# ScalarE forms the modulated norm in place with scale and shift, VectorE multiplies and subtracts 512 wide

## The chip, the core and the metric

The kernel runs on one core of a Trainium2 chip. The metric is the device time of one execution in microseconds, the median of several runs. The engines that matter here: TensorE multiplies matrices, VectorE and ScalarE work element by element on tiles of 128 partitions, and SyncE issues the transfers from memory. They run side by side and wait for each other through semaphores.

## What is computed

Two transformer blocks. The first has six sublayers ("subs" 0 to 5: feed-forward, differential attention, feed-forward, feed-forward, grouped attention, feed-forward), each of them on 256 tokens of `x` and, but for the last, 256 tokens of a context. Every sub begins with the same operation, and this is the one that is changed:

```python
def rmsnorm(x, g):
    xf = x.astype(jnp.float32)
    y = xf * lax.rsqrt(jnp.mean(xf * xf, axis=-1, keepdims=True) + NORM_EPS)
    return (y * g.astype(jnp.float32)).astype(x.dtype)

def modulated_norm(h, g, m, k):
    return rmsnorm(h, g) * (1.0 + m[..., k + 1, :]) + m[..., k, :]

def half_ffn(h, m, k, g_pre, g_post, w_in, w_out):
    y = swiglu(modulated_norm(h, g_pre, m, k), w_in, w_out)
    return gated_residual(h, y, g_post, m, k, 0.5)
```

`m` comes from the condition of `x` or of the context, so scale and shift differ between the two halves of the tokens. A second block of two layers follows; its norms have code of their own.

## The kernel before

Activations lie with the 1024 features on partitions, in eight chunks (KC) of 128, and the tokens along the row: 512 (TT), of which the first 256 (S) are `x` and the others the context. `hT` is the residual stream, `uT` the norm's product, `rstd` the root's inverse for each token, `modA` the columns of scale (norm weight times one plus the scale), `modt` the columns of shift. Each f32 matrix product is made of three with operands split into a high and a low part: `u_hi` with `w_hi`, `u_lo` with `w_hi`, `u_hi` with `w_lo` (lines 407 to 409). Weights stream through a ring of four slots; ScalarE makes `w_hi` of each half slot (line 943), VectorE `w_lo` (line 1354), and this frees the slot for SyncE. Two halves of weights ("columns") are ready before a sub begins.

The order of the work is written out by hand, engine by engine, and a sub starts like this. ScalarE squares `hT`, TensorE sums the squares (line 491), ScalarE makes `rstd` (lines 934 and 935). Then VectorE in `pre` walks over pieces of 256 tokens: it writes `uT` as `hT` times `modA` times `rstd` (line 1380) and, three pieces behind, `u_lo` as `uT` plus shift minus `u_hi` (line 1369). Scale and shift are different for `x` and context, hence two pieces a chunk. ScalarE in `modulate` writes `u_hi` as `uT` plus shift, rounded (line 976). TensorE in `two_columns` takes chunk by chunk for two columns of weights at once, and waits for each chunk's `u_lo`: 48 products. Subs 0 to 3 form and multiply all 512 tokens, sub 4 forms 512 but multiplies the first 256 in these two columns, sub 5 has 256 tokens only and one piece a chunk. After `modulate` ScalarE goes on with `w_hi` and the sub's own work, VectorE with `w_lo` and the condition's products (line 1342).

Of the kernel before, what the change touches and what calls it, by code (L numbers as in the profile page):

```python
# [7 lines left out]
F32 = mybir.dt.float32  # L8
F32R = mybir.dt.float32r
ACT = mybir.ActivationFunctionType  # L10
ALU = mybir.AluOpType
# [4 lines left out]
KC = D // P  # L16
S = 256
TT = 2 * S
DEPTH = 2
# [101 lines left out]
        _n += _w  # L121
NTABS, NHTABS = sum(TABS.values()), sum(HTABS.values())

T_READY_END = 5 * 2 * KC + KC + KC * (DEPTH + 1)

ADDED = KC - 3

# [6 lines left out]
def program(nc, wk, x_in, cols_in, crow_in, tabs_in, htabs_in, trig_in, uk_in, uv_in, out):  # L134
    with ExitStack() as ctx:
        def sem(name):
            return ctx.enter_context(nc.semaphore(name))
# [6 lines left out]
        def place(region, name, cols, dtype=F32):  # L144
            t = nc.alloc_sbuf_tensor_at(name, [P, cols], dtype, offset=at[region])
            at[region] += (cols * 4 + 31) // 32 * 32
            return t
# [5 lines left out]
        hT = place("fixed", "hT", KC * TT)  # L153
# [8 lines left out]
        modt = place("fixed", "modt", 6 * 48)  # L162
        modA = place("fixed", "modA", 6 * 16)
        modC = place("fixed", "modC", 6 * 16)
        small = place("fixed", "small", 256)
        rstd = place("fixed", "rstd", TT)
# [4 lines left out]
        u_hi = place("first", "u_hi", KC * TT, F32R)  # L171
        u_lo = place("first", "u_lo", KC * TT, F32R)
        uT = place("first", "uT", KC * TT)
# [88 lines left out]
        mod_ready = sem("mod_ready")  # L262
# [2 lines left out]
        ss_done = sem("ss_done")  # L265
        rstd_ready = sem("rstd_ready")
        t_ready = sem("t_ready")
        u_ready = sem("u_ready")
        ulo_ready = sem("ulo_ready")
        hhi_ready = sem("hhi_ready")  # L270
# [47 lines left out]
        def half_hi(h, a, b):  # L318
            n = (h % NW) * HALF
            return w_hi[:, n + a:n + b]  # L320

        def half_lo(h, a, b):
            n = (h % NW) * HALF
            return w_lo[:, n + a:n + b]
# [22 lines left out]
        def _(sp):  # L347
# [44 lines left out]
            assert n == NSLOTS  # L392
            sp.wait_ge(t_ready, T_READY_END)
            sp.dma_start(out, uT[:, 0:KC * S]).then_inc(out_done, 16)
# [3 lines left out]
        def _(pe):  # L398
# [6 lines left out]
            def three(bank, hi, lo, x_hi, x_lo, first, last):  # L405

                mm(bank, hi, x_hi, start=first, stop=False)  # L407
                mm(bank, hi, x_lo, start=False, stop=False)  # L408
                return mm(bank, lo, x_hi, start=False, stop=last)  # L409

            def weights(h):
                pe.wait_ge(wlo_ready, h + 1)

            def bank_a():

                nonlocal a
                if a >= 2:
                    pe.wait_ge(a_free, a - 1)
                a += 1
                return bankA[(a - 1) % 2]  # L420

            def bank_v():

                nonlocal v
                if v >= 2:
                    pe.wait_ge(v_free, v - 1)
                v += 1
                return bankV[(v - 1) % 2]

            def column(bank, T, xh, xl, stride, ready=None, seen=0, per=1):  # L430

                nonlocal H
                for k in range(KC):
                    if ready is not None:
                        pe.wait_ge(ready, seen - (KC - 1 - k) * per)
                    at_k = slice(k * stride, k * stride + T)
                    last = three(bank[:, 0:T], half_hi(H, k * P, (k + 1) * P), half_lo(H, k * P, (k + 1) * P),
                                 xh[:, at_k], xl[:, at_k], k == 0, k == KC - 1)
                last.then_inc(half_done, 1)
                H += 1  # L440
# [19 lines left out]
            def two_columns(banks, T, xh, xl, stride, ready, seen, per=1):  # L460

                nonlocal H
                weights(H + 1)
                for k in range(KC):
                    pe.wait_ge(ready, seen - (KC - 1 - k) * per)
                    at_k = slice(k * stride, k * stride + T)
                    for b in range(2):
                        last = three(banks[b][:, 0:T], half_hi(H + b, k * P, (k + 1) * P),
                                     half_lo(H + b, k * P, (k + 1) * P), xh[:, at_k], xl[:, at_k], k == 0, k == KC - 1)
                        if k == KC - 1:  # L470
                            last.then_inc(half_done, 1)
                H += 2
# [26 lines left out]
                    norm_term(c, T, ready, seen, src, stride)  # L499

            def ffn_in(T, f):
                two_columns([bank_a(), bank_v()], T, u_hi, u_lo, TT, ulo_ready, ulo_seen, T // S)
                for j in range(1, FT):
                    weights(H)
                    column(bank_a(), T, u_hi, u_lo, TT)
                    weights(H)
                    column(bank_v(), T, u_hi, u_lo, TT)
# [144 lines left out]
            for sub in range(6):  # L652
                T = S if sub == 5 else TT
                norm_sum(T, sq_ready, sq_seen)
                sq_seen += KC
                ulo_seen += KC * (T // S)
                if sub in FFN_SUBS:
                    f = FFN_SUBS.index(sub)
                    ffn_in(T, f)
                    ffn_out(T)  # L660
                    continue
                first = a
                two_columns([bank_a(), bank_a()], S if sub == 4 else T, u_hi, u_lo, TT, ulo_ready, ulo_seen, T // S)
                if sub == 1:
                    project(14, TT)
                    for s in range(4):
# [29 lines left out]
                else:  # L696
# [3 lines left out]
                    for t in range(10):  # L700
                        w = S if t < 8 else TT
                        n = t * S if t < 8 else GA_K + (t - 8) * TT
# [6 lines left out]
                    for t in range(10):  # L709
                        n = t * S if t < 8 else GA_K + (t - 8) * TT  # L710
# [209 lines left out]
        def _(act):  # L920
            f = nc.scalar.activation
# [45 lines left out]
                rms_inverse(rstd[:, 0:T], bankN[:, 0:T], D).then_inc(rstd_ready, 1)  # L967

            def modulate(sub, T):
                nonlocal t_seen  # L970
                for c in range(KC):
                    for s in range(T // S):
                        t_seen += 1
                        act.wait_ge(t_ready, t_seen)
                        piece = slice(c * TT + s * S, c * TT + (s + 1) * S)
                        f(u_hi[:, piece], uT[:, piece], ACT.Identity,
                          bias=modt[:, sub * 48 + 2 * c + s:sub * 48 + 2 * c + s + 1]).then_inc(u_ready, 1)

            def ffn(T, nth):
                nonlocal a, v, hid  # L980
# [106 lines left out]
            for sub in range(6):  # L1087
                T = S if sub == 5 else TT
                squares(T, h_ready if sub else None, h_seen - KC, 1)
                if sub == 0:  # L1090
# [5 lines left out]
                    high()  # L1096
                norm(T)
                modulate(sub, T)
                if sub == 0:
                    high()  # L1100
# [73 lines left out]
            for lay in range(DEPTH):  # L1174
# [78 lines left out]
                for h in range(SB_HEADS + 1):  # L1253
                    n = 8 * lay + h
# [14 lines left out]
                  scale=-1.0).then_inc(b2["mx"], 1)  # L1269
# [26 lines left out]
        def _(dve):  # L1296
            ts, tt, stt = nc.vector.tensor_scalar, nc.vector.tensor_tensor, nc.vector.scalar_tensor_tensor
            H = K = a = v = parts = 0
            steps = norms = 0
            t_n = u_n = rots = hns = units = hids = 0  # L1300
# [57 lines left out]
            def pre(sub, T):  # L1358
                nonlocal norms, t_n, u_n
                norms += 1  # L1360
                dve.wait_ge(mod_ready, sub + 1)
                dve.wait_ge(rstd_ready, norms)

                def low_part(j):
                    c, s = divmod(j, T // S)
                    dve.wait_ge(u_ready, u_n + j + 1)
                    piece = slice(c * TT + s * S, c * TT + (s + 1) * S)
                    shift = modt[:, sub * 48 + 2 * c + s:sub * 48 + 2 * c + s + 1]
                    stt(u_lo[:, piece], uT[:, piece], shift, u_hi[:, piece].bitcast(F32),  # L1369
                        ALU.add, ALU.subtract).then_inc(ulo_ready, 1)  # L1370

                behind = 3
                pieces = KC * (T // S)
                for j in range(pieces):
                    c, s = divmod(j, T // S)
                    if j >= behind:
                        low_part(j - behind)
                    n = c * TT + s * S
                    k = sub * 16 + 2 * c + s
                    stt(uT[:, n:n + S], hT[:, n:n + S], modA[:, k:k + 1], rstd[:, s * S:(s + 1) * S],  # L1380
                        ALU.mult, ALU.mult).then_inc(t_ready, 1)
                    t_n += 1
                for j in range(pieces - behind, pieces):
                    low_part(j)
                u_n += pieces

            def post(sub, T):
                nonlocal norms, yrs
# [177 lines left out]
            for sub in range(6):  # L1566
                T = S if sub == 5 else TT
                pre(sub, T)
                if sub == 0:
                    low()  # L1570
# [36 lines left out]
                else:  # L1607
                    lows(8 + 2 + 2)
                    dve.wait_ge(trig_ready, 32)
                    for t in range(10):  # L1610
                        w = S if t < 8 else TT
                        n = t * S if t < 8 else GA_K + (t - 8) * TT
                        b = (t % 2) * TT
                        head_norm(mix[:, n:n + w], col("gaq" if t < 8 else "gak"), hr[:, b:b + w])
                    for t in range(10):
                        n = t * S if t < 8 else GA_K + (t - 8) * TT
# [17 lines left out]
            for lay in range(DEPTH):  # L1634
# [7 lines left out]
                behind = 2  # L1642
# [261 lines left out]
            for c in range(KC):  # L1904
                stt(uT[:, c * S:(c + 1) * S], tile(hT, c), col("final", c), rstd[:, 0:S],
                    ALU.mult, ALU.mult).then_inc(t_ready, 1)
                t_n += 1
            assert t_n == T_READY_END
            assert H == K == HALVES
# [194 lines left out]
```

## Time and profile before

| | us |
|---|---|
| median of 3 runs | 2709.39 (2707.68 to 2712.68) |
| profiled execution | 2700.16 |
| its span | 2698.4 |
| TensorE busy in the span | 2490.8 (92%) |
| VectorE busy | 1612.1 (60%) |
| ScalarE busy | 1042.0 (39%) |
| mean granted TensorE clock | 0.961 of full speed |

The profiled execution is one run, recorded by the profiler; the span is the time from its first to its last instruction. Busy shares are means over stages that have different limits. A timeline gives for each instruction its start, its duration, and in brackets how long the engine was idle before it and what ended that. The duration of an instruction is longer than its place in a row of like ones, since the next starts before it has ended.

### The profile page before, as it was taken

To read this page: it belongs to the slowest core of one execution; us is meant where nothing else is said; L and a number is where in the kernel's file an instruction comes from. 1 tells how busy PE (TensorE), PEld (TensorE's weight loads), DVE (VectorE), ACT (ScalarE), POOL (GpSimd) and SP (SyncE) were. 2 spreads that over 40 slices of the span, in tenths; PEclk is the share of its full clock that TensorE was granted. 3 is DMA by queue.
4 is the path that set the end of the run, shared out by engine and by line. 5 is a ranking of instruction groups with operands and counts; after the bars stand their busy time and mean duration, and the time that the engine had idled before them with its cause. 6 is when DMAs were issued, how large, how long until landed. Compare 5 with 4: busy or idle time off the path is not lost.

```text
span 2698.4 us, 35057 instructions
## 1 busy us (share of the span) xinstructions
PE 2490.8 (92%) x14142; PEld 2105.3 (78%) x14142; DVE 1612.1 (60%) x2827; ACT 1042.0 (39%) x1739; POOL 0.2 (0%) x4
## 2 busy tenths in 40 slices
PE   6999998987899999899999888998998878998968
PEld 5888886874678888688888668998988658998658
DVE  8767755268477673676233655556466367466466
ACT  3222324247432223422232545445444434544433
POOL 0000000000000000000000000000000000000000
PEclk9999999989999999999999989999999879999879
DMA  6544441210135543145222203553544104534202
GB/s 267 209 190 187 187 156 63 89 53 1 67 135 197 197 189 125 47 187 203 94 94 98 90 32 116 188 188 141 183 140 170 63 16 143 209 141 156 79 1 95
DMA packets 48689, 349.72 MB, mean 130 GB/s; under 512 B 5392, under 2 KB 5520, under 8 KB 6544
## 3 DMA queue, kind: packets, MB, share of 16 engines
q1 hardware_dynamic: 48528, 347.48, 34.8%
q8 instruction: 113, 1.85, 0.3%
q14 instruction: 48, 0.39, 0.0%
HBM read 346.41 MB, written 1.05 MB: 129 GB/s over the span
## 4 chain that ended last, share of the span: by engine, by line
PE 84%; DVE 10%; ACT 3%; issue 2%; DMA 1%; SPq 0%; DVEq 0%; ACTq 0%
PE ps L407 24%; PE ps L409 24%; PE ps L408 24%; PE ps L491 1%; PE ps L571 1%; PE ps L573 1%; PE ps L572 1%; PE ps L614 1%; DVE small L1516 1%; DVE w_lo L1354 1%; PE ps L601 1%; DVE conv L1715 1%; ACT w_hi L943 1%; DVE yT L1394 1%; PE ps L794 1%
## 5 line engine op out<-in xcount | busy, mean ns | idle before, releaser
L943 ACT ACTIVATE w_hi<-ring 128x1024 fp32r<-128x1024 f32 x504 | 533.8, 1060 | 1261.4 <-PE ps L409 1187.4
L1354 DVE TENSOR_TENSOR w_lo<-ring,w_hi 128x1024 fp32r<-128x1024 f32 x504 | 616.6, 1224 | 634.9 <-ACT w_hi L943 632.7
L407 PE MATMUL ps<-u_hi,w_hi 128*128 128x512 f32 (+1 forms) x1744 | 631.7, 362 | 29.6 <-DVE u_lo L1369 27.2
L409 PE MATMUL ps<-u_hi,w_lo 128*128 128x512 f32 (+1 forms) x1744 | 635.1, 364 | 0.0
L408 PE MATMUL ps<-u_lo,w_hi 128*128 128x512 f32 (+1 forms) x1744 | 632.9, 363 | 0.0
L407 PEld LDWEIGHTS ps<-u_hi,w_hi 128*128 128x128 f32 x1744 | 330.3, 189 | 89.2 <-issue 32.6
L408 PEld LDWEIGHTS ps<-u_lo,w_hi 128*128 128x128 f32 x1744 | 330.3, 189 | 56.0 <-issue 0.5
L409 PEld LDWEIGHTS ps<-u_hi,w_lo 128*128 128x128 f32 x1744 | 330.2, 189 | 48.8
L407 PE MATMUL ps<-uh,w_hi 128*128 128x256 f32 x1184 | 336.5, 284 | 30.2 <-ACT zt L1231 17.0
L1342 DVE CUSTOM_DVE_ANT_0 waste<-ring,condb,cols 128x1024 f32<-128x1024 f32 x280 | 346.5, 1279 | 8.2 <-DMA ring<-in_wk 8.2
L408 PE MATMUL ps<-ul,w_hi 128*128 128x256 f32 x1184 | 333.1, 281 | 0.0
L409 PE MATMUL ps<-uh,w_lo 128*128 128x256 f32 x1184 | 333.1, 281 | 0.0
L409 PE MATMUL ps<-h_hi,w_lo 128*128 128x512 f32 (+1 forms) x704 | 257.2, 365 | 0.0
L407 PE MATMUL ps<-h_hi,w_hi 128*128 128x512 f32 (+1 forms) x704 | 255.8, 363 | 0.5 <-DVE h_lo L1426 0.5
L408 PE MATMUL ps<-h_lo,w_hi 128*128 128x512 f32 (+1 forms) x704 | 256.1, 364 | 0.0
L407 PEld LDWEIGHTS ps<-uh,w_hi 128*128 128x128 f32 x1184 | 225.7, 191 | 36.7 <-DVE w_lo L1354 20.0
L408 PEld LDWEIGHTS ps<-ul,w_hi 128*128 128x128 f32 x1184 | 225.9, 191 | 0.0
L409 PEld LDWEIGHTS ps<-uh,w_lo 128*128 128x128 f32 x1184 | 225.9, 191 | 0.0
L1440 DVE TENSOR_TENSOR hidden<-ps,hidden 128x512 f32<-128x512 f32 (+1 forms) x88 | 55.0, 625 | 202.9 <-PE ps L409 202.9
L407 PEld LDWEIGHTS ps<-h_hi,w_hi 128*128 128x128 f32 x704 | 132.1, 188 | 23.8 <-issue 0.9
L408 PEld LDWEIGHTS ps<-h_lo,w_hi 128*128 128x128 f32 x704 | 132.1, 188 | 23.8 <-issue 0.7
L409 PEld LDWEIGHTS ps<-h_hi,w_lo 128*128 128x128 f32 x704 | 132.3, 188 | 19.7
(274 smaller groups left out, 2711.1 us busy)
## 6 DMA issues: line engine op xcount, KB each, us to landing
ring<-in_wk SPq DMA_DIRECT2D x324, 1024.0 KB, 4.8
hT<-in_x SPq DMA_DIRECT2D x1, 2048.0 KB, 17.7
htabs<-in_htabs SPq DMA_DIRECT2D x1, 1152.0 KB, 7.2
condb<-in_crow SPq DMA_DIRECT2D x1, 1024.0 KB, 5.2
out_t<-uT SPq DMA_DIRECT2D x1, 1024.0 KB, 3.9
trig<-in_trig SPq DMA_DIRECT2D x3, 256.0 KB, 5.0
wuk<-in_uk SPq DMA_DIRECT2D x2, 256.0 KB, 5.2
wuv<-in_uv SPq DMA_DIRECT2D x2, 256.0 KB, 5.4
```

What stands on the lines that cost most here:

```text
L407: mm(bank, hi, x_hi, start=first, stop=False)
L408: mm(bank, hi, x_lo, start=False, stop=False)
L409: return mm(bank, lo, x_hi, start=False, stop=last)
L491: last = mm(bankN[:, 0:T], tab("ones"), src[:, c * stride:c * stride + T], start=c == 0, stop=c == KC - 1)
L571: mm(bank, x_h, half_hi(h, n, n + 256), start=k == 0, stop=False)
L572: mm(bank, x_l, half_hi(h, n, n + 256), start=False, stop=False)
L573: last = mm(bank, x_h, half_lo(h, n, n + 256), start=False, stop=k == KC - 1)
L601: last = nc.tensor.transpose(ps[5 + u % 2][:, kt * P:(kt + 1) * P], specs[u]["prob"](u % 2, kt), tab("ident"))
L943: f(half_hi(K, 0, HALF), ringed(n, K % 2 * HALF, (K % 2 + 1) * HALF), ACT.Copy).then_inc(whi_ready, 1)
L1342: last = nc.vector.tensor_tensor_reduce(waste[:, c * D:(c + 1) * D], ringed(slot, t * D, (t + 1) * D), condb[:, c * D:(c + 1) * D], 1.0, c ...
L1354: tt(half_lo(K, 0, HALF), ringed(HALF_SLOT[K], K % 2 * HALF, (K % 2 + 1) * HALF), half_hi(K, 0, HALF).bitcast(F32), ALU.subtract).then_inc ...
L1440: tt(h, bankV[v % 2][:, 0:T], h, ALU.mult).then_inc(v_free, 1)
```

## The change

ScalarE now does the whole affine step: for each piece of 256 it writes `uT` in place, scale times `uT` plus shift, and one chunk behind it copies the 512 of a chunk into `u_hi`, rounded. VectorE multiplies `hT` by `rstd` for a whole chunk and, two chunks behind, subtracts `u_hi` from `uT` for a whole chunk. A new semaphore `u_whole` keeps ScalarE's copy behind its own pieces. TensorE's waits count chunks instead of pieces. In sub 5 a chunk is 256 wide, so there the number of ScalarE's instructions doubles and VectorE's stays.

```diff
-T_READY_END = 5 * 2 * KC + KC + KC * (DEPTH + 1)
+T_READY_END = 6 * KC + KC * (DEPTH + 1)
...
-                two_columns([bank_a(), bank_v()], T, u_hi, u_lo, TT, ulo_ready, ulo_seen, T // S)
+                two_columns([bank_a(), bank_v()], T, u_hi, u_lo, TT, ulo_ready, ulo_seen)
...
-                ulo_seen += KC * (T // S)
+                ulo_seen += KC
...
             def modulate(sub, T):
+
                 nonlocal t_seen
-                for c in range(KC):
-                    for s in range(T // S):
+                act.wait_ge(mod_ready, sub + 1)
+                for c in range(KC + 1):
+                    if c < KC:
                         t_seen += 1
                         act.wait_ge(t_ready, t_seen)
-                        piece = slice(c * TT + s * S, c * TT + (s + 1) * S)
-                        f(u_hi[:, piece], uT[:, piece], ACT.Identity,
-                          bias=modt[:, sub * 48 + 2 * c + s:sub * 48 + 2 * c + s + 1]).then_inc(u_ready, 1)
+                        for s in range(T // S):
+                            piece = slice(c * TT + s * S, c * TT + (s + 1) * S)
+                            k = 2 * c + s
+                            f(uT[:, piece], uT[:, piece], ACT.Identity, bias=modt[:, sub * 48 + k:sub * 48 + k + 1],
+                              scale=modA[:, sub * 16 + k:sub * 16 + k + 1]).then_inc(u_whole, 1)
+                    if c:
+
+                        act.wait_ge(u_whole, sub * 2 * KC + c * (T // S))
+                        chunk = slice((c - 1) * TT, (c - 1) * TT + T)
+                        f(u_hi[:, chunk], uT[:, chunk], ACT.Copy).then_inc(u_ready, 1)
...
-                def low_part(j):
-                    c, s = divmod(j, T // S)
-                    dve.wait_ge(u_ready, u_n + j + 1)
-                    piece = slice(c * TT + s * S, c * TT + (s + 1) * S)
-                    shift = modt[:, sub * 48 + 2 * c + s:sub * 48 + 2 * c + s + 1]
-                    stt(u_lo[:, piece], uT[:, piece], shift, u_hi[:, piece].bitcast(F32),
-                        ALU.add, ALU.subtract).then_inc(ulo_ready, 1)
-
-                behind = 3
-                pieces = KC * (T // S)
-                for j in range(pieces):
-                    c, s = divmod(j, T // S)
-                    if j >= behind:
-                        low_part(j - behind)
-                    n = c * TT + s * S
-                    k = sub * 16 + 2 * c + s
-                    stt(uT[:, n:n + S], hT[:, n:n + S], modA[:, k:k + 1], rstd[:, s * S:(s + 1) * S],
-                        ALU.mult, ALU.mult).then_inc(t_ready, 1)
-                    t_n += 1
-                for j in range(pieces - behind, pieces):
-                    low_part(j)
-                u_n += pieces
+                def low_part(c):
+                    dve.wait_ge(u_ready, u_n + c + 1)
+                    chunk = slice(c * TT, c * TT + T)
+                    tt(u_lo[:, chunk], uT[:, chunk], u_hi[:, chunk].bitcast(F32), ALU.subtract).then_inc(ulo_ready, 1)
+
+                behind = 2
+                for c in range(KC + behind):
+                    if c < KC:
+                        n = c * TT
+                        tt(uT[:, n:n + T], hT[:, n:n + T], rstd[:, 0:T], ALU.mult).then_inc(t_ready, 1)
+                        t_n += 1
+                    if c >= behind:
+                        low_part(c - behind)
+                u_n += KC
```

ScalarE at the start of sub 0, before: from the root (`rstd`) over the sixteen pieces of `u_hi` to the next weights.

```order
L934 ACTIVATE rstd<-ps,cols 128x512 [waits ss_done]
L935 ACTIVATE rstd<-rstd 128x512 [waits act_step]
L976 ACTIVATE u_hi<-uT,modt 128x256 [waits t_ready] x16
L943 ACTIVATE w_hi<-ring 128x1024 [waits w_ready2]
L981 ACT_TABLE_LOAD
```

The same place of the changed kernel; the group of two pieces and a copy stands there six times more where the dots are.

```order
L935 ACTIVATE rstd<-ps,cols 128x512 [waits ss_done]
L936 ACTIVATE rstd<-rstd 128x512 [waits act_step]
L981 ACTIVATE uT<-uT,modt,modA 128x256 [waits t_ready,mod_ready]
L981 ACTIVATE uT<-uT,modt,modA 128x256
L981 ACTIVATE uT<-uT,modt,modA 128x256 [waits t_ready]
L981 ACTIVATE uT<-uT,modt,modA 128x256
L987 ACTIVATE u_hi<-uT 128x512 [waits u_whole]
...
L987 ACTIVATE u_hi<-uT 128x512 [waits u_whole] x2
L944 ACTIVATE w_hi<-ring 128x1024 [waits w_ready2]
```

The first `u_hi` was the first instruction behind the root; now it is the fifth.

VectorE at the same place, before: the end of the weights' low parts, then products and low parts in turn.

```order
L1354 TENSOR_TENSOR w_lo<-ring,w_hi 128x1024 [waits whi_ready] x2
L1380 SCALAR_TENSOR_TENSOR uT<-hT,modA,rstd 128x256 [waits mod_ready,rstd_ready,x_ready,dve_step]
L1380 SCALAR_TENSOR_TENSOR uT<-hT,modA,rstd 128x256 x2
L1369 SCALAR_TENSOR_TENSOR u_lo<-uT,modt,u_hi 128x256 [waits u_ready]
L1380 SCALAR_TENSOR_TENSOR uT<-hT,modA,rstd 128x256
```

And in the changed kernel:

```order
L1364 TENSOR_TENSOR w_lo<-ring,w_hi 128x1024 [waits whi_ready] x2
L1383 TENSOR_TENSOR uT<-hT,rstd 128x512 [waits mod_ready,rstd_ready,x_ready,dve_step]
L1383 TENSOR_TENSOR uT<-hT,rstd 128x512 x2
L1377 TENSOR_TENSOR u_lo<-uT,u_hi 128x512 [waits u_ready]
L1383 TENSOR_TENSOR uT<-hT,rstd 128x512
```

The pattern is the same, three products ahead of the first low part, but each instruction is a chunk of 512 and no longer a piece of 256.

## Rows read from the trace of the kernel before

**Rows 1.** The page: the span, and the engines' shares of the last chain.

```profile
span 2698.4 us, 35057 instructions
...
PE 84%; DVE 10%; ACT 3%; issue 2%; DMA 1%; SPq 0%; DVEq 0%; ACTq 0%
```

**Rows 2.** Waits: who waited for whom, us in total, times, longest.

```profile
PE ps L407 <- DVE u_lo L1369: 27.2, 10, 5.5
```

**Rows 3.** Timeline of sub 1: start, duration, engine, line, out<-in, count [idle before].

```profile
429.44 1.28 DVE L1380 SCALAR_TENSOR_TENSOR uT<-hT,modA,rstd 128x256 f32<-128x256 f32 x3 [1.33 <-ACT rstd L935]
429.96 1.30 ACT L976 ACTIVATE u_hi<-uT,modt 128x256 fp32r<-128x256 f32 x3 [0.63 <-DVE uT L1380]
...
431.42 0.48 DVE L1369 SCALAR_TENSOR_TENSOR u_lo<-uT,modt,u_hi 128x256 fp32r<-128x256 f32 x1
...
432.05 0.47 PE L407 MATMUL ps<-u_hi,w_hi 128*128 128x512 f32 x1 [4.11 <-DVE u_lo L1369]
...
434.16 0.63 PE L407 MATMUL ps<-u_hi,w_hi 128*128 128x512 f32 x1
...
435.44 0.63 PE L407 MATMUL ps<-u_hi,w_hi 128*128 128x512 f32 x1
...
436.47 0.40 PE L407 MATMUL ps<-u_hi,w_hi 128*128 128x512 f32 x1
...
440.93 1.27 DVE L1369 SCALAR_TENSOR_TENSOR u_lo<-uT,modt,u_hi 128x256 fp32r<-128x256 f32 x3
...
444.03 0.39 PE L407 MATMUL ps<-u_hi,w_hi 128*128 128x512 f32 x1
444.23 1.06 ACT L943 ACTIVATE w_hi<-ring 128x1024 fp32r<-128x1024 f32 x1 [2.68 <-PE ps L409]
```

**Rows 4.** TensorE by stretches of sub 1: stretch, length, busy, granted clock, DMA.

```profile
429.40:432.70 3.30, 0.65 (x3) 1.00 0.55 233
432.80:436.10 3.30, 3.30 (x9) 0.50 0.00 0
436.20:444.70 8.50, 8.50 (x38) 1.00 0.01 2
```

**Rows 5.** Timeline of VectorE: two 512-wide multiplies by the root.

```profile
730.41 1.29 DVE L1394 TENSOR_TENSOR yT<-yT,rstd 128x512 f32<-128x512 f32 x2 [2.55 <-ACT rstd L935]
```

**Rows 6.** ScalarE by line: ns min/median/max, first and last start; then a timeline row.

```profile
L976 ACT ACTIVATE u_hi<-uT,modt x88: 492/509/512, 44.4 to 1672.1; 128x256 fp32r<-128x256 f32 x88
...
L1183 ACT ACTIVATE uh<-conv x16: 416/418/419, 1870.1 to 2287.0; 128x256 fp32r<-128x256 f32 x16
...
L1203 ACT ACTIVATE pad<-ps x16: 363/365/368, 1928.0 to 2357.7; 128x256 f32<-128x256 f32 x16
...
L1035 ACT ACTIVATE yT<-ps,modC x24: 456/458/471, 686.3 to 1655.1; 128x256 f32<-128x256 f32 x24
...
L1125 ACT ACTIVATE u_hi<-uT x8: 612/612/632, 671.4 to 682.8; 128x512 fp32r<-128x512 f32 x8
...
686.29 0.82 ACT L1035 ACTIVATE yT<-ps,modC 128x256 f32<-128x256 f32 x2
```

**Rows 7.** Timeline of sub 4: first piece, last low parts, the last two chunks' products.

```profile
1514.31 1.28 DVE L1380 SCALAR_TENSOR_TENSOR uT<-hT,modA,rstd 128x256 f32<-128x256 f32 x3 [1.32 <-ACT rstd L935]
...
1525.79 1.28 DVE L1369 SCALAR_TENSOR_TENSOR u_lo<-uT,modt,u_hi 128x256 fp32r<-128x256 f32 x3
...
1526.34 0.38 PE L407 MATMUL ps<-u_hi,w_hi 128*128 128x256 f32 x1 [0.61 <-DVE u_lo L1369]
...
1527.15 0.37 PE L407 MATMUL ps<-u_hi,w_hi 128*128 128x256 f32 x1
```

**Rows 8.** Timeline around sub 5: 256-wide multiplies, first piece, first product.

```profile
1657.63 0.76 DVE L1394 TENSOR_TENSOR yT<-yT,rstd 128x256 f32<-128x256 f32 x2 [1.12 <-ACT rstd L935]
...
1666.86 1.27 DVE L1380 SCALAR_TENSOR_TENSOR uT<-hT,modA,rstd 128x256 f32<-128x256 f32 x3 [3.77 <-ACT rstd L935]
...
1668.68 0.55 PE L407 MATMUL ps<-u_hi,w_hi 128*128 128x256 f32 x1 [2.88 <-DVE u_lo L1369]
```

More of the change, by code:

```diff
@@ L267, in program @@
         t_ready = sem("t_ready")
+        u_whole = sem("u_whole")
         u_ready = sem("u_ready")
@@ L662, in _ @@
                 first = a
-                two_columns([bank_a(), bank_a()], S if sub == 4 else T, u_hi, u_lo, TT, ulo_ready, ulo_seen, T // S)
+                two_columns([bank_a(), bank_a()], S if sub == 4 else T, u_hi, u_lo, TT, ulo_ready, ulo_seen)
                 if sub == 1:
```

## The prediction

> **What bounds the kernel now.** I read the chain that ended last first: TensorE carries 84% of it and VectorE 10% [rows 1], so a change on ScalarE and VectorE counts only where TensorE stands and waits for them. The table of waits then says where that is for this code: TensorE waited for `u_lo` (line 1369) ten times, 27.2 us in all, the longest 5.5 us [rows 2]. That is the whole stake of the change: six norms ("subs" 0 to 5), each with a start-up before TensorE's first product, and nothing else.
>
> The timeline of sub 1 shows one such start-up [rows 3]. Take T0 = 429.44, when VectorE starts its first piece of `uT`. Sixteen pieces of `uT` and sixteen of `u_lo`, each 256 wide, follow each other; from the second `u_lo` (431.42) to the fourteenth (440.93) are 24 places in 9.51 us, 0.396 us a place, 1.58 us a chunk of 512. TensorE's first product needs both halves of chunk 0: the second `u_lo` ends at 431.42 + 0.48 = 431.90 and the product starts at 432.05, so T0 + 2.61, 0.15 us behind its input. From there on TensorE never waits in subs 0 to 3: it works through 48 products without a gap. Three products take 435.44 - 434.16 = 1.28 us at a granted clock of 0.50, 0.427 each; 33 products take 444.03 - 436.47 = 7.56 us at full clock, 0.229 each, or 1.37 us a chunk [rows 3, 4]. The clock stood at 1.2 GHz for a stretch just after the start, following the 4.11 us in which TensorE idled, and at 2.4 GHz before and after [rows 3, 4]. ScalarE had 2.68 us of idle time when the two columns ended [rows 3]: what it does later is covered, its first results are not.
>
> **The change, part by part.** The norm's multiply on VectorE: before 2 x 256 wide, now one instruction of 512. The like of it is `yT<-yT,rstd`, two in 1.29 us, one of them some 0.69: a place of 0.60 [rows 5]. `u_lo` becomes an instruction of the same kind and size. VectorE so needs 1.20 us a chunk for 1.58; over the program 176 places of 0.396 give way to 80 of 0.60 and, in sub 5, 16 of 0.34 (two in 0.76 [rows 8]), 69.7 us to 53.4, 16 less. All of that is idle time won, since VectorE no longer sets the pace.
>
> ScalarE before: two pieces a chunk, `Identity` with the shift as a column from memory, 0.509 us each. After: two pieces with two such columns (shift and scale), written in place, and a plain copy of 512, which takes 0.612 [rows 6]. No row has an instruction with both columns. Rows have each alone: a bias column makes 0.418 (plain, SBUF to SBUF) into 0.509, +0.091; a scale column makes 0.365 (plain, from PSUM) into 0.458, +0.093 [rows 6]. If they add, a piece takes 0.60; if the second comes free, 0.51. Back to back such instructions overlap: two of 0.458 end after 0.82, so the place is 0.36, 0.096 less than the duration [rows 6]. The place of a new piece is then 0.50, or 0.41 (taken as 0.40) if the second column is free, and that of the copy 0.52. I take 0.50, since each column shows its own increment and no row shows one that came without; 0.40 stays for the range.
>
> The Trainium skill (ScalarE: Activation LUTs, What ACT_TABLE_LOAD costs) says that each pointer operand adds about 93 ns, and gives no discount for a second. The trace agrees for each alone and shows no pair. By that rule the change costs the 6.5 us below; without it, the 4.0 us of the first rival.
>
> Start-up of a 512-wide sub, from T0: VectorE's first multiply 0.68, hand-over to ScalarE 0.04 (429.44 to 429.96 is 0.52 with a piece of 0.48 [rows 3]), so ScalarE starts at 0.72. It now makes the two pieces of chunk 0, and, as the loop is written, the two of chunk 1 before the copy of chunk 0: 0.72 + 4 x 0.50 = 2.72. The copy ends at 3.33, VectorE starts the subtraction at 3.37 (its own third multiply is over at 1.9), ends at 4.06, and TensorE starts at 4.21. Before it was 2.61: **1.60 us later**. With 0.40 the same sum gives 3.81, 1.20 later.
>
> Pace behind it: ScalarE 2 x 0.50 + 0.52 = 1.52 us a chunk, TensorE 1.37 at best. The last chunk's `u_lo` comes at 4.21 + 6 x 1.52 + 0.60 = 13.93. VectorE's loop keeps two chunks behind: copy c lets it subtract (0.65 after the copy's start), then multiply chunk c+3 (0.60 and 0.72 more), 1.97 in all; ScalarE wants that at 2.04. The new loop just holds with 0.50; with 0.40 it sets 1.39 a chunk.
>
> *Subs 0 to 3* (512 wide, TensorE never out of input). Starting 1.60 later costs 1.60 if the clock's slow stretch moves along. If the stretch stays where it is, TensorE misses 1.60 us of slow time, 3.7 products at 0.427, and makes them up at full clock: 3.7 x 0.229 = 0.85. So 0.85 to 1.60 each, 1.22 taken; four subs: **+4.9** (3.4 to 6.4).
>
> *Sub 4* forms 512 but multiplies only 256 wide, so TensorE is faster than its input there and waits (0.61 us before the seventh chunk); the last chunk's products start at 1527.15, T0 + 12.84 [rows 7]. Now 13.93: **+1.1**. With 0.40: 3.81 + 6 x 1.39 + 0.60 = 12.75, -0.1. This is the one place where the faster VectorE could pay, and at 0.50 it doesn't.
>
> *Sub 5* (256 wide, one piece a chunk): TensorE started at T0 + 1.82 [rows 8]. Now the multiply takes 0.42, ScalarE starts at 0.46, two pieces to 1.46, copy 0.42, hand-over 0.04, subtraction 0.42, and 0.15: 2.49, **0.67 later**, 0.37 of it left if the slow stretch stays; 0.5 taken. With 0.40: 0.47 later, 0.35 taken.
>
> The new wait on `u_whole` asks for the chunk before the one just formed, whose pieces ended at least two pieces earlier; `mod_ready` VectorE awaits itself ahead of its first multiply, so it is there by then. Queued behind the `u_whole` wait is ScalarE's copy alone, and VectorE and TensorE wait for that copy anyway. I put both waits at nothing. If the wait took the overlap of 0.1 from each copy, sub 4 would lose 0.7 more and the others 0.1 each. DMA queues are not touched: the ring is released by `w_lo`, and its order is unchanged.
>
> Sum: 4.9 + 1.1 + 0.5 = 6.5 us on the profiled 2700.16, so 2706.7; the three timed runs have a median of 2709.39 with the same program, hence **2715.9 us**. Within this case the ends are 3.4 + 1.1 + 0.4 = 4.9 and 6.4 + 1.1 + 0.7 = 8.2: 2714.3 to 2717.6.
>
> **Rivals.** *The second column is free* (0.40 a piece). 1.20 later in subs 0 to 3, between 0.64 and 1.20 each: 3.7; sub 4 -0.1; sub 5 +0.35; sum 4.0, **2713.4 us**, no difference that can be told. For it: nothing in the rows excludes that two columns are fetched together. Against: the two increments are equal and each is the full one.
>
> *More slow clock.* TensorE's idle time before its first product grows from 4.11 us to 5.7 us in subs 0 to 4, and a slow stretch costs (0.427 - 0.229) x 8 products, 1.6 us, where it lies on products. Three to five more of these, here or in the gaps further on that the delay shifts, give 6.5 + 4.8 to 8.0: 2720.7 to 2723.9, say **2722 us**. For it: every start-up seen has such a stretch after its idle time. Against: one longer gap need not make two.
>
> *Faster, by less slow clock elsewhere.* The same program gave 2700.16 us profiled and 2707.68 to 2712.68 timed; something of that size moves with where the idle gaps fall. If the new spacing removed slow stretches, each gives 1.6 us back; the point is at 5 of them (6.5 us) for no change and 8 for faster by 0.2%: **2703 us**. Within the six norms themselves nothing can do that: the least the change costs there is zero, as the last chunk comes no sooner than before unless a piece's place is under 0.40. I see no row that speaks for so many.
>
> **How the numbers follow.** The forecast gets 0.55, the free column 0.2, more slow clock 0.2, less 0.05. What a measurement can tell from no change is about 0.2%, 5.4 us. The forecast's own span lies to nine tenths above 2714.8; part of it falls under that line with the spread of the medians, some 2 us. Slower: 0.55 x 0.7 + 0.2 x 0.3 + 0.2 x 0.95, 0.63, put at 0.6; faster 0.04; same 0.36. The range runs from the free column with its stretches at the low end and a median 1.5 us low (2709.5) to more slow clock (2723).
>
> **What would show it.** In the changed profile: ScalarE's piece 0.60 (0.51 in the first rival), first `uT` to first product 4.2 us in subs 0 to 4 (before 2.61), ScalarE's place a chunk 1.52; VectorE's busy time some 16 us lower; TensorE's wait for `u_lo` at about 27 + 5 x 1.6 + 0.7 = 36 us; its clock lines for the number of slow stretches. I am wrong if the piece takes 0.51 or if the spans of subs 0 to 3 grow by less than 0.8 us each, and in another way if the total moves by several us while these six places move as said: then it is the clock.

## The result

The changed kernel takes 2715.66 us (median of 13 runs, 2713.34 to 2719.29); the kernel before, in 13 runs, 2707.68 us. The ratio is 1.0031 with a 95% interval of 1.0021 to 1.0042: slower by 8.4 us (5.7 to 11.4). Beside the first experiments below, on one chip with them, the same file came out at 1.0043 (1.0024 to 1.0061). The forecast was 2715.9 us, slower. How much of that nearness is luck stands below, in the part on the prediction.

Behind what follows stand two profiled executions, 2700.16 us of before (span 2698.4) and 2713.34 us of after (span 2711.6). That of before lies 7.5 us under its median, so their difference of 13.2 us is more than the 8.0 of the medians. Their stages can be compared, their totals less so.

The page of the changed kernel, counterpart of [rows 1]: span, busy time by engine, and the shares of the last chain.

```profile
span 2711.6 us, 35031 instructions
...
PE 2492.2 (92%) x14142; PEld 2109.5 (78%) x14142; DVE 1599.1 (59%) x2747; ACT 1065.7 (39%) x1787; POOL 0.2 (0%) x4
...
PE 84%; DVE 9%; ACT 4%; issue 2%; DMA 1%; SPq 0%; DVEq 0%; ACTq 0%
```

VectorE is busy 13.0 us less than before, ScalarE 23.7 us more, and the chain has moved a point from the one to the other. The waits of the changed kernel (us in total, times, longest), counterpart of [rows 2]:

```profile
PE ps L408 <- DVE u_lo L1377: 35.3, 8, 7.6
DVE u_lo L1377 <- ACT u_hi L987: 18.7, 39, 1.5
ACT uT L981 <- DVE uT L1383: 7.0, 6, 2.8
```

TensorE waits 8.1 us longer for `u_lo`. VectorE, which never waited for `u_hi` before, does so 39 times now, while ScalarE waits for `uT` only at the six starts: ScalarE sets the pace. The timeline of sub 1, counterpart of [rows 3]:

```profile
431.45 1.90 DVE L1383 TENSOR_TENSOR uT<-hT,rstd 128x512 f32<-128x512 f32 x3 [1.31 <-ACT rstd L936]
432.23 2.08 ACT L981 ACTIVATE uT<-uT,modt,modA 128x256 f32<-128x256 f32 x4 [0.89 <-DVE uT L1383]
434.22 0.61 ACT L987 ACTIVATE u_hi<-uT 128x512 fp32r<-128x512 f32 x1
434.74 1.08 ACT L981 ACTIVATE uT<-uT,modt,modA 128x256 f32<-128x256 f32 x2
434.86 0.69 DVE L1377 TENSOR_TENSOR u_lo<-uT,u_hi 128x512 fp32r<-128x512 f32 x1 [1.52 <-ACT u_hi L987]
...
435.70 0.76 PE L408 MATMUL ps<-u_hi,w_hi 128*128 128x512 f32 x1 [5.74 <-DVE u_lo L1377]
435.72 0.61 ACT L987 ACTIVATE u_hi<-uT 128x512 fp32r<-128x512 f32 x1
```

T0 is 431.45. Four pieces stand ahead of the first copy, which starts at 434.22, T0 + 2.77; VectorE has waited 1.52 us for it; the first product starts at T0 + 4.25 where it was T0 + 2.61. The next copy starts at 435.72: 1.50 us a chunk.

What this is worth at the end of each norm is in the next table. The first column of each pair is the start of TensorE's first product, the second the end of the 48th (its start plus its duration), both from T0.

| sub | before | after | first later by | 48th later by |
|---|---|---|---|---|
| 0 | 2.61, 15.69 | 4.25, 17.63 | 1.64 | 1.94 |
| 1 | 2.61, 15.45 | 4.25, 16.98 | 1.64 | 1.53 |
| 2 | 2.61, 15.44 | 4.26, 18.10 | 1.65 | 2.66 |
| 3 | 2.61, 15.43 | 4.25, 17.04 | 1.64 | 1.61 |
| 4 | 2.61, 13.78 | 4.25, 14.88 | 1.64 | 1.10 |
| 5 | 1.82, 9.12 | 2.53, 11.11 | 0.71 | 1.99 |

The six sum to 10.8 of the spans' 13.2 us. The rest lies in the other work: from T0 of sub 1 to T0 of sub 2 the changed kernel takes 314.68 us for 314.28, though its norm costs 1.53, so there 1.1 us came back; between the norms of subs 4 and 5 it loses 1.3 us more than sub 4's norm costs, and behind the norm of sub 5 another 2.2. Two single profiles can't say whether these pieces belong to the change.

In subs 0, 2 and 5 the loss is larger than the later start. Sub 2 of the changed kernel on TensorE, by stretches (length, busy, granted clock, DMA), counterpart of [rows 4], and its products:

```profile
746.20:749.60 3.40, 0.00 (x0) 0.94 0.01 2
750.50:755.20 4.70, 4.70 (x11) 0.50 0.00 0
755.40:764.00 8.60, 8.60 (x38) 0.97 0.00 0
```

```profile
750.39 0.76 PE L408 MATMUL ps<-u_hi,w_hi 128*128 128x512 f32 x1 [5.74 <-DVE u_lo L1377]
...
755.22 0.63 PE L410 MATMUL ps<-u_hi,w_lo 128*128 128x512 f32 x1
755.64 0.57 PE L408 MATMUL ps<-u_hi,w_hi 128*128 128x512 f32 x1
...
763.84 0.39 PE L410 MATMUL ps<-u_hi,w_lo 128*128 128x512 f32 x1
```

The first twelve products, 750.39 to 755.64, ran at 1.2 GHz, 0.44 us each; before it were about eight [rows 3, 4]. The later start fell into a slow stretch that went on for longer. Sub 5 shows the same thing, before and after:

```profile
1668.70:1671.70 3.00, 3.00 (x14) 0.50 0.00 0
1672.00:1676.00 4.00, 4.00 (x36) 1.00 0.02 4
```

```profile
1678.60:1684.20 5.60, 5.60 (x27) 0.50 0.00 0
1684.60:1687.00 2.40, 2.40 (x23) 1.00 0.03 7
```

Before, the clock was up again by 1672.00, T0 + 5.1; after, it was still down at 1684.20, T0 + 8.3. How long the lower level lay on the 48 products follows from their length and mean granted clock (twice the length times what the mean lacks of 1): in subs 0 to 3 some 4.0, 3.4, 3.4 and 3.4 us before, 4.6, 2.9, 5.6 and 3.4 after, and in sub 5 3.1 and 6.0.

### The profile page after: what moved, and what is told of

It is laid out like the page before. It is cut to its first block, busy times and chain, and to the rows that moved or that the text cites. A ratio compares the mean times of both kernels' runs of the same rounds, so it can differ in the third digit from the quotient of the medians.

```text
span 2711.6 us, 35031 instructions
## 1 busy us (share of the span) xinstructions
PE 2492.2 (92%) x14142; PEld 2109.5 (78%) x14142; DVE 1599.1 (59%) x2747; ACT 1065.7 (39%) x1787; POOL 0.2 (0%) x4
## 3 DMA queue, kind: packets, MB, share of 16 engines
HBM read 346.41 MB, written 1.05 MB: 128 GB/s over the span
## 4 chain that ended last, share of the span: by engine, by line
PE 84%; DVE 9%; ACT 4%; issue 2%; DMA 1%; SPq 0%; DVEq 0%; ACTq 0%
PE ps L408 24%; PE ps L410 24%; PE ps L409 23%; PE ps L492 2%; PE ps L572 1%; PE ps L574 1%; PE ps L573 1%; PE ps L615 1%; DVE small L1518 1%; PE ps L602 1%; DVE w_lo L1364 1%; DVE conv L1717 1%; ACT w_hi L944 1%; PE ps L795 1%; ACT uT L981 1%
## 5 line engine op out<-in xcount | busy, mean ns | idle before, releaser
L408 PE MATMUL ps<-u_hi,w_hi 128*128 128x512 f32 (+1 forms) x1744 | 636.0, 365 | 37.7 <-DVE u_lo L1377 35.3
```

## The experiments

The theory: the change costs what TensorE's first product comes later at the start of each norm, with what the clock makes of it, and in sub 4 what the last chunk comes later. The first rival: ScalarE's pace or its longer work costs it. The second: each start tips the clock. Ratios are to the kernel before on the same chip; a thousandth is 2.7 us.

**The yardstick.** The changed file itself.

> The changed kernel once more, beside the others on the same chip. Theory 'start-up' (the change costs what TensorE's first product comes later in the six norms, and what the clock makes of it): +8 us on the kernel before, first product at T0 + 4.25 in subs 0 to 4. It is the yardstick for the others; no rival differs here.

1.0043 (1.0024 to 1.0061), +11.6 us (6.5 to 16.5), for 8 expected; first product at T0 + 4.25 in subs 0 to 4. The 48th products ended 2.41, 1.62, 2.72, 1.53, 1.10 and 1.96 us later than in the profile of before, 11.3 in all.

**The order of ScalarE's first three steps.**

```diff
-                    if c:
-                        act.wait_ge(u_whole, sub * 2 * KC + c * (T // S))
-                        chunk = slice((c - 1) * TT, (c - 1) * TT + T)
+                    for d in ([0] if c == 0 else [] if c == 1 else [c - 1]):
+                        act.wait_ge(u_whole, sub * 2 * KC + (d + 1) * (T // S))
+                        chunk = slice(d * TT, d * TT + T)
                         f(u_hi[:, chunk], uT[:, chunk], ACT.Copy).then_inc(u_ready, 1)
```

> The change, but ScalarE copies chunk 0 right behind its own two pieces instead of behind those of chunk 1; all later chunks as in the change. Theory 'start-up': the copy starts at T0 + 1.9 instead of 2.77, TensorE's first product at T0 + 3.4 instead of 4.25 in subs 0 to 4, 2.15 instead of 2.53 in sub 5; sub 4, which waits for its last chunk, gains nothing. 0.4 to 0.9 us less in subs 0 to 3 and 0.3 in sub 5: 2 to 4 us less than the change, +4 to +6 on before. Rival 'pace' (ScalarE's 1.5 us a chunk sets TensorE's progress): nothing gained, +8.

1.0021 (1.0006 to 1.0036), +5.7 us: 6 less than the yardstick, where 2 to 4 were expected, with intervals that overlap. Its timeline in sub 1:

```profile
431.46 1.89 DVE L1382 TENSOR_TENSOR uT<-hT,rstd 128x512 f32<-128x512 f32 x3 [1.66 <-ACT rstd L936]
432.24 1.09 ACT L981 ACTIVATE uT<-uT,modt,modA 128x256 f32<-128x256 f32 x2 [0.89 <-DVE uT L1382]
433.37 0.63 ACT L986 ACTIVATE u_hi<-uT 128x512 fp32r<-128x512 f32 x1
...
434.87 0.76 PE L408 MATMUL ps<-u_hi,w_hi 128*128 128x512 f32 x1 [4.90 <-DVE u_lo L1376]
```

The copy starts at T0 + 1.91, the first product at T0 + 3.41. In sub 4 the 48th product ended at 15.01 (14.88 in the change): an earlier start gains nothing where the last chunk decides. The six 48th products ended 1.67, 1.08, 0.91, 0.95, 1.23 and 1.56 us later than before, 7.4 in all for the yardstick's 11.3. That is 3.9 us less and inside the expected band; the difference of the medians alone would not carry it. The same instructions do the same work here, at the same pace; only the start differs, and the norms follow it. That speaks against the first rival, for which nothing would have been gained. The pace is not far away, though: in subs 2 and 3 of this run TensorE waited for `u_lo` at the seventh chunk (in sub 2 its weight load stood 0.28 us), so with this ScalarE loop the 48th product comes no sooner than about T0 + 16.35. In the four wide norms of the changed kernel's profile TensorE didn't wait once behind its first product: there the start decides.

**The second column.**

```diff
-                            f(uT[:, piece], uT[:, piece], ACT.Identity, bias=modt[:, sub * 48 + k:sub * 48 + k + 1],
-                              scale=modA[:, sub * 16 + k:sub * 16 + k + 1]).then_inc(u_whole, 1)
+                            f(uT[:, piece], uT[:, piece], ACT.Identity, bias=modt[:, sub * 48 + k:sub * 48 + k + 1]).then_inc(u_whole, 1)
```

> The change without the scale column in ScalarE's pieces (bias column only): the multiplication by norm weight and scale is left out of the computation. Theory 'each column has its own price': the piece falls from 0.587 to 0.51 us and its place from 0.49 to 0.41; first product at T0 + 3.9; sub 4's last chunk at 12.8 instead of 13.9, now set by VectorE's loop at 1.39 us a chunk. About 2 us less than the change, +6 on before. If both columns shared a price, the piece would stay at 0.587 and nothing would move.

This kernel leaves out the multiplication by norm weight and scale. 1.0032 (1.0020 to 1.0043), +8.7 us for 6 expected; beside the yardstick 3 less, within both intervals. The piece itself is clear. With both columns (the changed kernel), and with the shift's alone; columns are ns min/median/max, first and last start:

```profile
L981 ACT ACTIVATE uT<-uT,modt,modA x88: 583/587/602, 44.8 to 1682.1; 128x256 f32<-128x256 f32 x88
```

```profile
L981 ACT ACTIVATE uT<-uT,modt x88: 491/493/512, 44.7 to 1683.0; 128x256 f32<-128x256 f32 x88
```

The second column costs 0.094 us, as much as the first did in [rows 6]: they add. The first product came at T0 + 3.87 and sub 4's 48th ended at 13.85, 0.07 later than before. The other subs did not show it: 0.76, 2.30, 1.05, 2.35 and, in sub 5, 1.88 us later than before, with more slow clock in subs 1 and 3 (5.7 us of it on the 48 products for 3.4 before). This run settles the price of the instruction, not that of the program.

**The later start alone.** The kernel before, VectorE held ahead of its first piece; twice in the second file.

```diff
                 dve.wait_ge(rstd_ready, norms)
+                for wide in (512, 512, 64)[:3 if T == TT else 1] * 1:
+                    step(tt(u_lo[:, 7 * TT:7 * TT + wide], hT[:, 7 * S:7 * S + wide], rstd[:, 0:wide], ALU.mult))
```

> The kernel before with VectorE held up ahead of its first piece of every norm: three scratch multiplies (512, 512 and 64 wide, each awaited, about 1.6 us) in subs 0 to 4, one (0.7 us) in sub 5. Nothing of the change is in it. Theory 'start-up': TensorE's first product 1.6 us later as in the change, in sub 4 all 1.6 count: +8 to +10 on before, the change's loss to within 2 us. Rival 'pace' or 'ScalarE's longer work': at most the part of the start-up that products in the slow stretch don't absorb, under +4.

> As e3_later_once with twice the hold: about 3.2 us ahead of every norm in subs 0 to 4 and 1.4 us in sub 5, in all 17.6 us. Theory 'start-up, us for us, the clock averaged out': twice what e3_later_once cost (ratio 1.0055, 14.9 us), but no more than the hold plus some two slow stretches of 1.6 us: +15 to +21 on before. Rival 'a later start tips the clock': one more slow stretch in each of six norms, +25 or more. Rival 'products absorb it': under +10.

The hold in sub 1, once:

```profile
431.09 1.68 DVE L1364 TENSOR_TENSOR u_lo<-hT,rstd 128x512 fp32r<-128x512 f32 x3 [1.32 <-ACT rstd L935]
432.81 1.28 DVE L1382 SCALAR_TENSOR_TENSOR uT<-hT,modA,rstd 128x256 f32<-128x256 f32 x3
...
435.42 0.76 PE L407 MATMUL ps<-u_hi,w_hi 128*128 128x512 f32 x1 [5.81 <-DVE u_lo L1371]
```

It was 432.81 - 431.09 = 1.72 us, with 0.7 in sub 5 some 9.3 in all. Measured: once 1.0055 (1.0035 to 1.0076), +14.9 us (9.5 to 20.5); twice 1.0089 (1.0072 to 1.0105), +24.0 us (19.5 to 28.4). Both medians lie above the expected bands, 8 to 10 and 15 to 21; both intervals reach into them. By the medians the second hold added 9.1 us for 9.3 held, which the two intervals leave open by several us. The first added some 5 more than its length, though 9.5, the interval's low end, is next to none; in its profile the 48th products ended, beyond the hold, 0.11, 1.17, 1.13, -0.14, 0.01 and 1.31 us later, 3.6 in all, by the clock (in subs 1 and 2 it was down for 6.0 and 5.9 us of the 48 products, before for 3.4). In the profile of twice the hold they ended 0.10, 0.39, 0.37, 0.39, 0.01 and 0.62 us later beyond it, 1.9 in all: the longer idle time brought less slow clock into the norms than the shorter. The mean granted clock of the runs was 0.957 for once and 0.956 for twice, 0.960 and 0.961 for the kernel before beside them. So a later start, with nothing of the change in it, costs at least what it lasts. The change holds TensorE 1.64 us in five subs and 0.71 in the sixth, 8.9 us; with sub 4 at the 1.10 that its last chunk comes later it is 8.4. It costs 8.4 and 11.6: the hold explains it. ScalarE's added 23.7 us of work are not needed for it beyond the five steps ahead of the first product and, in sub 4, the pace. The second rival, a slow stretch for each start (+25 or more for twice), is not borne out as stated, but the interval of twice the hold, up to 28.4, reaches there.

**An earlier start.** The kernel before; of TensorE's first six products the four that need only `u_hi` go first.

```diff
+                    if k == 0:
+                        pe.wait_ge(u_ready, seen - (KC - 1) * per)
+                        for b in range(2):
+                            mm(banks[b][:, 0:T], half_hi(H + b, 0, P), xh[:, at_k], start=True, stop=False)
+                            mm(banks[b][:, 0:T], half_lo(H + b, 0, P), xh[:, at_k], start=False, stop=False)
+                        pe.wait_ge(ready, seen - (KC - 1) * per)
+                        for b in range(2):
+                            mm(banks[b][:, 0:T], half_hi(H + b, 0, P), xl[:, at_k], start=False, stop=False)
+                        continue
```

> The kernel before with another order of TensorE's first six products of every norm: the four that need only u_hi of chunk 0 start as soon as ScalarE has written it, the two with u_lo follow. Nothing else is changed. Theory 'start-up': first product at T0 + 1.6 instead of 2.61 in subs 0 to 4 and 1.2 instead of 1.82 in sub 5; the 48th product then ends no earlier than the last u_lo and one chunk allow, T0 + 14.3 instead of 15.4 in subs 0 to 3; sub 4 as before. 0.3 to 1.1 us less in each of subs 0 to 3 and 0.3 in sub 5: 2 to 5 us less than before. Rival: the clock falls as TensorE starts and takes it all, no difference.

1.0004 (0.9987 to 1.0021), +1.1 us (-3.5 to 5.7): no difference that can be told, the rival's forecast, for 2 to 5 us less expected; a gain of up to 3.5 is not excluded. The first product came at T0 + 1.57, 1.04 us earlier, and the 48th ended at 15.55, 15.53, 15.06, 15.62, 13.80 and 8.63, where before had 15.69, 15.45, 15.44, 15.43, 13.78 and 9.12. Sub 1 (T0 = 429.53) by stretches, and its first product with those where the pace changes:

```profile
431.10:434.40 3.30, 3.30 (x8) 0.50 0.00 0
434.60:435.60 1.00, 1.00 (x4) 0.50 0.00 0
...
440.00:444.50 4.50, 4.50 (x22) 1.00 0.00 0
```

```profile
431.10 0.77 PE L469 MATMUL ps<-u_hi,w_hi 128*128 128x512 f32 x1 [3.07 <-ACT u_hi L985]
...
436.36 0.63 PE L407 MATMUL ps<-u_hi,w_hi 128*128 128x512 f32 x1
436.79 0.49 PE L408 MATMUL ps<-u_lo,w_hi 128*128 128x512 f32 x1
437.11 0.39 PE L409 MATMUL ps<-u_hi,w_lo 128*128 128x512 f32 x1
```

The products ran slowly from the first one on, until the one at 436.79 was under way: 5.9 us at half clock, where before the slow stretch lay between 432.8 and 436.2, 3.4 us [rows 3, 4]. The granted clock was back at 1.00 from T0 + 7.5 on, before from T0 + 6.8. The 1.04 us, and a little more, were spent on products at half speed. Subs 0 and 3 show the same.

Sub 2 doesn't, and it shows a second reason. Its granted clock was 1.00 from the first product to the last (745.7 to 759.3), and still its 48th product ended only 0.38 us sooner than before. T0 is 744.17; the lines are the first product, the first of the second chunk, the first of the seventh with its weight load (PEld), and the 48th:

```profile
745.74 0.47 PE L469 MATMUL ps<-u_hi,w_hi 128*128 128x512 f32 x1 [3.06 <-ACT u_hi L985]
...
748.27 0.50 PE L407 MATMUL ps<-u_hi,w_hi 128*128 128x512 f32 x1 [0.85 <-DVE u_lo L1378]
...
756.20 0.19 PEld L407 LDWEIGHTS ps<-u_hi,w_hi 128*128 128x128 f32 x1 [0.36 <-DVE u_lo L1378]
756.20 0.50 PE L407 MATMUL ps<-u_hi,w_hi 128*128 128x512 f32 x1
...
758.84 0.39 PE L409 MATMUL ps<-u_hi,w_lo 128*128 128x512 f32 x1
```

TensorE waited for `u_lo` at every chunk from the second to the seventh, 7.93 us for five chunks or 1.59 each, which is VectorE's pace [rows 3]. So in subs 1 to 3 of the kernel before an earlier start can bring no more than 0.4 us each, and 0.6 in sub 0, even with the clock up all the time: the pieces come no faster. The expected T0 + 14.3 left this out; the last two chunks, 12 products, can't start before the seventh chunk's `u_lo`, here at T0 + 12.03. The clock alone, as the rival had it, is not the whole cause.

**Where the pieces bind most.** In sub 4 TensorE waits for pieces it does not yet multiply: its first eight columns take only the 256 tokens of `x`. The next file, on top of the last, makes the eight pieces of `x` first and the context's eight later, two behind each of four tiles; the core of the edit, with VectorE's loop in the same order:

```diff
-                modulate(sub, T)
+                modulate(sub, T, halves=[0] if sub == 4 else None)
...
-                    tiles(8, qk_tile)
+                    for m in range(8):
+                        tiles(1, lambda t, bank, m=m: qk_tile(m, bank))
+                        if 1 <= m <= 4:
+                            modulate(sub, T, (2 * m - 2, 2 * m - 1), [1])
...
                     project(6, S)
+                    pe.wait_ge(ulo_ready, ulo_seen)
                     project(2, TT)
```

> e5_high_products_first, and in sub 4 the eight pieces of the context, which TensorE first needs nine columns later, are made after the first two columns' results are taken out, two behind each of four tiles; the eight pieces of x come first. Theory 'sub 4 is bound by its pieces': the last chunk is there at T0 + 6.4 instead of 12.8 and the 48th product ends at about 9 instead of 13.8; ScalarE and VectorE keep up with the columns behind (2.8 us each). 3 to 5 us less than e5, 5 to 9 less than before. Rival: the pieces come back as waits in the later columns, no gain over e5.

0.9990 (0.9978 to 1.0001), 2.7 us less than before (5.9 less to 0.3 more), interval just touching none; 5 to 9 less were expected. Against e5 it is 3.8 less, for 3 to 5 expected. In the trace the gain is clear: sub 4's 48th product ended at T0 + 8.42 for 13.78, and the pieces fit between the tiles. ScalarE in sub 4 (T0 = 1514.64):

```profile
1519.91 0.51 ACT L989 ACTIVATE u_hi<-uT,modt 128x256 fp32r<-128x256 f32 x1 [0.28 <-DVE uT L1399]
1522.74 1.06 ACT L956 ACTIVATE w_hi<-ring 128x1024 fp32r<-128x1024 f32 x1 [2.32 <-PE ps L409]
...
1528.98 0.90 ACT L989 ACTIVATE u_hi<-uT,modt 128x256 fp32r<-128x256 f32 x2
1530.21 1.06 ACT L956 ACTIVATE w_hi<-ring 128x1024 fp32r<-128x1024 f32 x1 [0.32 <-PE ps L409]
```

Behind the context's pieces ScalarE still waits 0.32 us for TensorE, so the columns are not held up. Two more runs, to part the two edits and to firm up the gain:

> The kernel before with the context's pieces of sub 4 made later (two behind each of four tiles) and nothing else; TensorE's first six products stand in their old order. Theory 'sub 4 is bound by its pieces, and an earlier first product buys nothing elsewhere': sub 4's 48th product ends at about T0 + 8.5 instead of 13.8, the other subs as before: 5 to 6 us less than before, the same as e6_context_later within 1 us. Rival 'the early products bring something on the average': e6 is better than this by 2 us or more.

> e6_context_later once more, beside e7_context_later_alone on one chip: 5 to 6 us less than before if sub 4's gain stands (first measured at ratio 0.9990, 0.9978 to 1.0001), with the high products first bringing nothing.

The context's pieces alone: 0.9984 (0.9967 to 1.0000), -4.3 us. Both edits again: 0.9975 (0.9963 to 0.9988), -6.8 us. Sub 4's 48th product ended at 8.00 and 9.93. Whether the early products add anything can't be told: the two intervals overlap, and e5 showed none; but both edits came out 2.5 us below the one, which is what the rival of that expectation asked for, and in subs 0 to 2 of the last profile the 48th product ended 0.62, 0.40 and 0.39 us sooner than before. The profile of the context's pieces alone, 2703.50 us for 2693.88 with both, is no measure of this: 6.9 us of it are another thing, told in the last section. The kernel with both edits beats the one before in its second measurement and is not clearly apart in its first; it beats the changed one in both.

## Why the prediction was right, step by step

- *Two columns add* (0.60 us, a place of 0.50): right. 0.587 us, two in 1.08, so a place of 0.49. The Trainium skill's rule (ScalarE: Activation LUTs, What ACT_TABLE_LOAD costs) holds for the pair, 0.094 for the second by e2. The first rival, a free column, is out.
- *Start-up 4.21*: 4.25 measured. The copy started at 2.77 for 2.72; the hand-over to ScalarE took 0.78 - 0.68 = 0.10 from VectorE's instruction, not 0.04.
- *Pace 1.52, set by ScalarE*: 1.50, and VectorE waits for it 39 times.
- *Subs 0 to 3, 0.85 to 1.60 each, 4.9 in all*: too low. They measured 1.94, 1.53, 2.66 and 1.61 in one profile, 7.7, and 8.3 in the yardstick. The idea that TensorE would lose slow time and make it up at full clock failed in three of the four. In sub 1 the clock was down for 0.5 us less of the products (2.9 us for 3.4), but the products behind came every 0.233 us instead of 0.229, and 1.53 of the 1.64 us remained; in sub 3 the slow stretch moved along, 3.4 us for 3.4; in subs 0 and 2 it went on over more products, 4.6 for 4.0 and 5.6 for 3.4.
- *Sub 4, +1.1*: 1.10 in both profiles.
- *Sub 5, +0.5*: the start was right (2.53 for 2.49), the loss 1.99, by the clock.
- *TensorE's wait of 36 us*: 35.3. *VectorE 16 us less*: 13.0. An instruction that had to wait no longer overlaps the one ahead, and 39 waits times the 0.08 us between duration and place (0.68 and 0.60) would make the 3 us.
- *The total*: 2715.9 for 2715.66 is in good part luck. The forecast stood on 2709.39, the median of three runs; the 13 runs of before gave 2707.68, 1.7 lower, and the difference was 8.4 us (8.0 by the medians) for 6.5 forecast, and the two errors cancel. In the profile the six norms cost 10.8 us for the 6.5: the term for subs 0 to 3 was too small by 2.8 us and that for sub 5 by 1.5, and the medians of two sets of runs, each spread over 6 to 14 us, do not resolve that.
- *More slow clock*, the second rival, was in part what happened: not three to five more stretches over the program, but longer ones in two of the norms. *Faster, by less slow clock elsewhere* did not come about.

## What to carry to other kernels

Where an engine is fed by a chain of small steps, look at what stands ahead of its first input, not at the producers' busy time: a wider instruction or a skewed loop that lowers busy time can put more work before the first result. An affine step that moves to ScalarE with scale and bias as columns pays for each column in each instruction (0.09 us each here), so small pieces make it dear. Before an earlier start is bought, look whether the producers could feed it: here they came every 1.58 us a chunk, and 1.04 us of earlier start was worth at most 0.4 to 0.6 a norm. And ask which of the pieces the waiting engine needs first; in sub 4 that brought the end of the first two columns 5.4 us forward, where a piece cheaper by 0.094 us brought the changed kernel 1.0.

## What the runs showed of the hardware that was not expected

- TensorE's clock made a later start cost its full length and more (e3: 14.9 us for 9.3 held, e4: 24.0 for 18.6, both with wide intervals). An earlier start brought nothing that can be told (e5: 1.04 us earlier in five norms, ratio 1.0004). In sub 1 the granted clock was back at 1.00 from T0 + 6.8 when the products began at T0 + 2.61, and from T0 + 7.5 when they began at T0 + 1.57: the earlier ones ran on the lower of the two levels. In sub 2 of the same run the clock never fell, after the same idle time (3.06 us for 3.07), and the pace of the pieces held TensorE back instead.
- Products had two paces at a granted clock of 1.00. In sub 1 of the changed kernel's profile the 512-wide ones came every 0.233 us behind the slow stretch, and in the long feed-forward stages of both profiles every 0.229. In the norm that is 0.2 us. In the profile of e7 it went on from the norm of sub 2 to 1115 us: between 751 and 1115 us 1562 products stand where the kernel before has 1580, both at a granted clock of 1.00, and from T0 of sub 2 to T0 of sub 3 it took 392.2 us for 385.3, though the norm itself cost 0.1. So the slower pace can cost 6.9 us of a run, almost as much as the change, and neither the granted clock nor the edit accounts for it. What causes it is open, and how many of the timed runs had it is not on record.
